# Normalisations of raw rows through a diagonal of row factors, chunk by chunk, and an attention pipeline one step deeper, in a two-block transformer kernel

## The reference

```python
def modulate(x, g, shift, scale):
    return rms_norm(x, g) * (1 + scale) + shift

h = modulate(x, lp["g_norm1"], sh1, sc1)
proj = h @ lp["w_in"]
...                       # two kinds of attention, a 2-D Fourier mix, sigmoid gates
x = x + gt1 * merge_branches(o_mla, o_gqa, o_four, proj[..., GATE_START:], lp)
x = x + gt2 * conv_ffn(modulate(x, lp["g_norm2"], sh2, sc2), lp)
```

## Time and profile before

| | us |
|---|---|
| median of 3 runs | 2947.84 (2944.81 to 2951.18) |
| profiled execution | 2950.79 |
| its span, first to last instruction | 2948.9 |
| TensorE busy | 2635.8 (89%) |
| VectorE busy | 1772.1 (60%) |
| ScalarE busy | 1445.4 (49%) |
| GpSimd busy | 631.0 (21%) |
| mean granted TensorE clock | 0.944 |

### The profile page before, as it was taken

How to read it: one execution, slowest core, us unless ns; L and a number is a source line. 1 busy time by engine, 2 the same in 40 slices (tenths; PEclk the granted TensorE clock), 3 DMA queues, 4 the chain that set the end, 5 groups by cost and what they waited for, 6 DMA issues and landing times.

```text
span 2948.9 us, 46949 instructions
## 1 busy us (share of the span) xinstructions
PE 2635.8 (89%) x17262; PEld 2293.7 (78%) x17262; DVE 1772.1 (60%) x2449; ACT 1445.4 (49%) x2194; POOL 631.0 (21%) x446
## 2 busy tenths in 40 slices
PE   5778998998998899769988999999799999988998
PEld 3547967987875799658667988978689789866996
DVE  5564756775674776657756765653556554455545
ACT  5453553663444376334444754444455454445544
POOL 0002203332211333231013323302023023111321
PEclk9787998998999999879998999999999999999999
DMA  8674514554540455434314656555246546532663
GB/s 298 205 255 125 159 58 143 170 173 130 174 129 14 138 172 185 121 97 141 104 56 127 188 187 192 187 178 179 85 125 195 173 157 188 191 129 75 183 195 126
DMA packets 332941, 450.47 MB, mean 153 GB/s; under 512 B 28192, under 2 KB 207392, under 8 KB 332768
## 3 DMA queue, kind: packets, MB, share of 16 engines
q1 hardware_dynamic: 332400, 446.58, 48.4%
q0 software_dynamic: 368, 1.57, 0.2%
HBM read 446.99 MB, written 1.05 MB: 152 GB/s over the span
## 4 chain that ended last, share of the span: by engine, by line
PE 78%; DVE 9%; ACT 5%; DMA 4%; issue 3%; POOL 1%; SPq 1%; DVEq 0%; ACTq 0%
PE S L780 24%; PE S L771 21%; PE G L780 14%; PE G L771 9%; DMA raw<-in_w_mod 4%; PE TB L828 3%; DVE wlo L574 2%; ACT whi L569 2%; PE S L857 2%; PE G L899 1%; ACT pp L1142 1%; POOL rs L1763 1%; DVE nmx L1552 1%; PE G L928 1%; PE S L928 1%
## 5 line engine op out<-in xcount | busy, mean ns | idle before, releaser
L574 DVE TENSOR_TENSOR wlo<-raw,whi 128x1024 fp32r<-128x1024 f32 x723 | 942.8, 1312 | 824.6 <-ACT whi L569 818.8
L569 ACT CAST whi<-raw 128x1024 fp32r<-128x1024 f32 x872 | 905.4, 1049 | 894.9 <-PE S L771 301.5
L780 PE MATMUL S<-hhi,whi 128*128 128x256 f32 x1952 | 547.3, 280 | 3.4 <-DVE wlo L574 1.6
L780 PE MATMUL S<-hhi,wlo 128*128 128x256 f32 x1952 | 546.5, 280 | 0.0
L780 PE MATMUL S<-hlo,whi 128*128 128x256 f32 x1952 | 546.2, 280 | 0.0
L574 POOL TENSOR_TENSOR wlo<-raw,whi 128x1024 fp32r<-128x1024 f32 x149 | 362.4, 2432 | 746.0 <-ACT whi L569 745.1
L780 PEld LDWEIGHTS S<-hhi,whi 128*128 128x128 f32 x1952 | 367.0, 188 | 5.3 <-issue 4.8
L780 PEld LDWEIGHTS S<-hlo,whi 128*128 128x128 f32 x1952 | 367.4, 188 | 0.2
L780 PEld LDWEIGHTS S<-hhi,wlo 128*128 128x128 f32 x1952 | 367.3, 188 | 0.0
L780 PE MATMUL G<-hhi,whi 128*128 128x256 f32 x1088 | 309.4, 284 | 16.7 <-DVE hlo L1279 15.0
L780 PE MATMUL G<-hlo,whi 128*128 128x256 f32 x1088 | 308.1, 283 | 0.0
(11 more groups left out here) (323 smaller groups left out, 4528.2 us busy)
## 6 DMA issues: line engine op xcount, KB each, us to landing
raw<-in_ffn_wi SPq DMA_DIRECT2D x352, 256.0 KB, 3.5
raw<-in_w_up SPq DMA_DIRECT2D x264, 256.0 KB, 3.3
raw<-in_w_mod SPq DMA_DIRECT2D x192, 256.0 KB, 3.7
raw<-in_w_in SPq DMA_DIRECT2D x192, 256.0 KB, 3.1
raw<-in_ffn_wo SPq DMA_DIRECT2D x160, 256.0 KB, 3.5
raw<-in_w_down SPq DMA_DIRECT2D x120, 256.0 KB, 3.3
raw<-in_a_wqkv SPq DMA_DIRECT2D x72, 256.0 KB, 3.0
raw<-in_w_o SPq DMA_DIRECT2D x48, 256.0 KB, 3.3
```

The lines of the kernel that those rows point to most:

```text
L569: act.copy(whi[:, n0 % SPLIT], raw[:, n0 % RAW]).then_inc(hi_done, 1)
L574: eng.tensor_tensor(wlo[:, n0 % SPLIT], raw[:, n0 % RAW], whi[:, n0 % SPLIT].bitcast(F32), ALU.subtract)\
L780: mm = pe.matmul(out_[:, m * T:(m + 1) * T], w, x, start=first and c == 0 and m == 0 and z == 0, stop=last and c == kc - 1 and z == len(te ...
```

## The change

The normalisations no longer scale rows before they are transposed. TensorE multiplies raw tiles of `resid` with a 128x128 diagonal of the row factors (`turn_rows`), which transposes and scales at once, into four banks. ScalarE takes out every chunk with scale and shift (`modulated`), VectorE does both parts of every split (`split_chunks`); `in` and the `up` of the first block wait for their chunks by twos. The squares are taken by ScalarE: over whole rows ahead of `in`, over half rows inside `wo1`. Where a `norm` follows a `down` (twice: latent 1 in layer 0, context 1 in layer 1), its whole work stands inside the second unit of that `down`: squares at slots 0 and 1, powers at 2, diagonals at 4, turning behind slots 5 to 8, modulating and splitting at slots 7 to 10. In attention the transposes follow three steps behind the scores (`TURN_LAG`), and the values of one step, 128 columns, four behind (`VALUE_LAG`); there are still three `prob` tiles.

```diff
-WARM_STEPS, WARM_PRODUCTS = 0, 6
+TURN_LAG, VALUE_LAG = 3, 4
...
+        def inner(st):
+            z = STAGES[STAGES.index(st) + 1] if st.kind == "down" and st.conv else None
+            return z if z and z.kind == "norm" else None
...
+        def split_with_norm(st, k, j, i, split, hooks):
+            for h in range(len(slot_shapes(st.kc))):
+                split(k, j, i, (h,))
+                if k == 1 and h in hooks:
+                    hooks[h]()
...
-            return st.kind in ("qkv", "pgate") or st.kind == "up" and not st.conv
+            return st.kind in ("in", "qkv", "pgate", "up")
...
+            def turn_rows(st, n):
+                pe.wait_ge(diag_done, NT * (st.ng + 1))
+                if n == 2:
+                    for b in range(2):
+                        wait_count(pe, bank_free[b], st.u + 2 - PAIRS)
+                for c in range(2):
+                    c0 = (2 * n + c) * P
+                    for t in range(NT):
+                        mm = pe.matmul(turned_banks(st)[n][:, c * T + t * P:c * T + (t + 1) * P], resid[st.s][:, t, c0:c0 + P],
+                                       diag2[:, t, :], start=True, stop=True, skip_group_check=True)
+                mm.then_inc(turned_done, 1)
...
+                        if st.kind == "down" and inner(st) and k == 1 and h in (5, 6, 7, 8):
+                            turn_rows(inner(st), h - 5)
...
-                for s in range(n + 3):
+                for s in range(n + VALUE_LAG):
                     if s < n:
                         scores(s)
...
-                    if 2 <= s < n + 2:
-                        turn(s - 2)
-                    if s >= 3 and s % 2 == 0:
-                        values((s - 4) // 2)
+                    if TURN_LAG <= s < n + TURN_LAG:
+                        turn(s - TURN_LAG)
+                    if s >= VALUE_LAG:
+                        values(s - VALUE_LAG)
...
-                    pe.wait_ge(rows_ready, st.rr + 2)
-                    for n in range(KD // 2):
-                        transposes(st.tk + n, [xn[:, t, c * P:(c + 1) * P] for c in (2 * n, 2 * n + 1) for t in range(NT)])
-                    wait_operand(st)
+                    if not inside(st):
+                        for n in range(KD // 2):
+                            turn_rows(st, n)
...
+            def row_squares(st, t):
+                act.activation(xn[:, t, :], resid[st.s][:, t, :], ACT.Square, scale=D ** -0.5,
+                               accum_out=ssq[:, t, 2:3]).then_inc(sq_done, 1)
+            def modulated(st, c):
+                scale, shift = modulation(st, c)
+                act.wait_ge(turned_done, st.nt + c // 2 + 1)
+                act.activation(unsplit[:, c, :], turned_banks(st)[c // 2][:, c % 2 * T:(c % 2 + 1) * T], ACT.Identity,
+                               scale=scale, bias=shift).then_inc(chunk_done, 1)
...
+                elif st.kind == "wo1":
+                    def half_squares(k, j, i):
+                        for b in range(2):
+                            act.wait_ge(half_ready, 4 * wo1s.index(st) + 2 * k + b + 1)
...
+                    hooks = {0: lambda: row_squares(z, 0), 1: lambda: row_squares(z, 1), 7: lambda: two(0),
+                             8: lambda: two(1), 9: lambda: two(2), 10: lambda: two(3)}
...
+            def row_diag(st, t):
+                dve.wait_ge(rs_ready, st.rq + t + 1)
+                dve.tensor_scalar(diag2[:, t, :], ident, rs[:, t, 0:1], None, ALU.mult).then_inc(diag_done, 1)
+            def split_chunks(st, n):
+                for c in (2 * n, 2 * n + 1):
+                    dve.wait_ge(chunk_done, norms.index(st) * KD + c + 1)
+                    dve.tensor_copy(hhi[:, c, :], unsplit[:, c, :]).then_inc(hhi_done, 1)
+                    dve.wait_ge(hhi_done, 2 * st.nt + c + 1)
+                    dve.tensor_tensor(hlo[:, c, :], unsplit[:, c, :], hhi[:, c, :].bitcast(F32), ALU.subtract).then_inc(hlo_done, 1)
...
-                        dve.tensor_tensor_reduce(scratch[:, :], x[:, t, :], x[:, t, :], 1.0 / D, EPS, ALU.mult, ALU.add,
-                                                 ms[:, t, 0:1]).then_inc(ms_ready, 1)
...
-                        dve.tensor_scalar(xn[:, t, :], x[:, t, :], rs[:, t, 0:1], None, ALU.mult).then_inc(rows_ready, 1)
...
+                        hooks = {2: pair(row_mean), 4: pair(row_diag), 7: lambda: split_chunks(z, 0), 8: lambda: split_chunks(z, 1),
+                                 9: lambda: split_chunks(z, 2), 10: lambda: split_chunks(z, 3)}
```

More of the change, by code:

```diff
@@ L529, in build, with inside, modulation @@
         last1 = [st for st in STAGES if st.kind == "down" and st.conv][-1]
+        wo1s = [st for st in STAGES if st.kind == "wo1"]
+        norms = [st for st in STAGES if st.kind == "norm"]
+        wides = [st for st in STAGES if st.kind == "up" and not st.conv]
+        def inner(st):
+            z = STAGES[STAGES.index(st) + 1] if st.kind == "down" and st.conv else None
+            return z if z and z.kind == "norm" else None
+        def inside(st):
+            return inner(STAGES[STAGES.index(st) - 1]) is st
+        def modulation(st, c):
+            w = int(st.which) - 1
+            return amul[:, st.l, w, c, st.s:st.s + 1], modT[:, st.l, 3 * w * KD + c, st.s:st.s + 1]
         def lo_by_pool(st, n0):
@@ L606, in turned @@
             outs = []
[L607 to L612, removed]
+            if st.kind == "ctrans":
                 outs = [(unsplit[:, c, :], col(f"gc{st.l}", c), None) for c in range(5 if st.full else 2)]
@@ L645, in parts_of @@
         def parts_of(st):
-            if st.kind not in ("norm", "ctrans"):
+            if st.kind != "ctrans":
                 return {}
@@ L1073, in _ @@
                             hi_operand(st, *split[q])
+                if st.kind == "norm" and not inside(st):
+                    if st.which == "1":
+                        for t in range(NT):
+                            row_squares(st, t)
+                    for c in range(KD):
+                        modulated(st, c)
                 if st.kind == "norm2":
@@ L1625, in gated @@
                             add = dve.tensor_tensor(x, x, tmp, ALU.add)
-                            if st is last1 and k == 1:
+                            if st.kind == "wo1":
+                                add.then_inc(half_ready, 1)
+                            elif st is last1 and k == 1:
                                 add.then_inc(rows_ready, 1)
@@ L1757, in _, with powers @@
                     pool.dma_start(pT[:, :, :, :], dram["pT"].rearrange("p (l c t) -> p l c t", l=DEPTH, c=2)).then_inc(ld_mask, 16)
-                for t in range(st.counts["rq"]):
+                def powers(st, t):
                     pool.wait_ge(ms_ready, st.rq + t + 1)
@@ L1763, in _ @@
                     pool.tensor_tensor(rs[:, t, w0:w0 + w], ms[:, t, w0:w0 + w], mhalf[:, 0:w], ALU.pow).then_inc(rs_ready, 1)
+                if not (st.kind == "norm" and inside(st)):
+                    for t in range(st.counts["rq"]):
+                        powers(st, t)
                 if st.counts["n"]:
@@ L1784, in _ @@
                                     lambda *at_: None, lambda *at_: None, chunks_lo)
+                    elif inner(st):
+                        z = inner(st)
+                        over_units(pool, st, lambda k, j, i: split_with_norm(
+                            st, k, j, i, lambda k, j, i, which: split_weights(st, j, i, k, lo, which),
+                            {2: lambda: [powers(z, t) for t in range(NT)]}))
                     else:
```

151 lines of the change are left out of this document (87 added, 64 removed).

## The result

The changed kernel takes 2862.1 us (median of four runs, 2859.0 to 2865.6) where the kernel before takes 2947.2: ratio 0.971, 95% interval 0.9694 to 0.9727, 2.9% less. Forecast were 2867 us, with a range of 2850 to 2897. The profiled execution took 2865.6 us (span 2863.8) against 2950.8 before, so 85.2 us went; 81.2 were forecast.

A forecast was written before the change was run, and what follows sets the result against it. TensorE, with 78% of the chain of waits, was taken to bound the kernel. 22.2 + 11.7 + 29.8 + 17.5 = 81.2 us off the profiled 2950.8 leaves 2869.6, or 2867 us against the median; range 2850 to 2897.

The forecast's parts named there:

- Outer normalisations: Normalisations 1, 2, 4, 6 and 7, outside a down projection: shorter stretches and a faster clock win 22.2 + 11.7 us.
- 12.5 of clock: Products right behind the outer normalisations no longer run at half clock: 7.7 us in 2, 4, 7 and 4.8 in 1, 6.
- the powers stay: In normalisations 2, 4, 7 GpSimd's two powers keep their 2.49 us; TensorE begins at 5.4 us instead of 7.2.
- Inner ones: Normalisations 3 and 5, moved inside a down projection: 13.3 and 16.5 us won, together 29.8.
- the queue on VectorE: Behind normalisation 3, chunks, weight subtractions and gated adds queue up, making a weight slot of the next product late: 2.6 us.
- that slot is GpSimd's own: 0.4: Behind normalisation 5 the fourth weight slot of the next product is GpSimd's, so only 0.4 us is lost.
- Attention: Turning one step deeper, values in halves: two latent stages win 12.7 us, dilated 2.3, window 2.0, context 0.5; 17.5 together.
- One: Outer normalisations: turning out of a standstill keeps the clock at 1.2 GHz; they give 18 instead of 34, 2883 us; chance 0.16.
- Two: VectorE late by the port lock: some 8 us in the down units, 1 in each outer normalisation; 2880 us; chance 0.12.
- Three: Attention gives nothing, as exponentials wait for the turning of three steps before: price 17.5, 2885 us; chance 0.12.
- four: Attention slower: a loop over one step makes wide steps 6.7 us instead of 3.9, 112 us more, 2997; chance 0.02.
- Five: Inner turning waits for its diagonal in the down unit: two more slots in each, 11 us, 2878 us; chance 0.02.

The follow-up runs named there:

- changed_again: The changed kernel unaltered, run once more beside later follow-up runs: 2859.9 us, ratio 0.9701 to the kernel before.
- wait_all: The changed kernel, but the product behind a first-block normalisation waits for all eight chunks, not two at a time: 2889.4 us, ratio 0.9808.
- attn_only: The kernel before with only the attention part of the change: 2928.3 us, ratio 0.9917.
- act_early: The changed kernel; behind an inner normalisation ScalarE waits for the gated products only ahead of its first evacuation, not its first weight split: 2861.6 us, ratio 0.9701.
- norm_only: The changed kernel with the old attention pipeline: 2888.9 us, ratio 0.9791 to the kernel before.
- transposed: The changed kernel with rows turned by transposes, one instruction for two, row factors left out of the result: 2851.9 us, ratio 0.9671.

## Why the prediction was right, and where not

**Outer normalisations**, 33.9 us forecast: 76.9 - 48.7 = 28.2 of stretches and the forecast 12.5 of clock, 40.7. The clock came back inside the turning as argued from the earlier trace rows. Mis-sized was TensorE's beginning: in 2, 4 and 7, 5.4 us was put for "the powers stay", with their 2.49 us, and it is 4.2. That duration came from the work beside them: begun at 486.71 in normalisation 2, two such powers would end at 489.2, and they end at 488.15. In 1 and 6, 4.9 and 4.1 were put, and it is 4.3 and 3.2. All this is worth 5.1 of the 6.8 us, a shorter turning (28.6 for 30.3) the rest.

**Inner ones**, 29.8 forecast: 16.9 + 18.0 + 4.9 of clock, less two turnings of 3.6 and the stalls of 2.7 and 2.9, 27.0. Behind 3 the queue on VectorE was forecast to 0.1 us (2.6), in part by luck: the 0.53 us that its subtraction then waited for ScalarE's split, in the row at 696.33, was not in the sum. Behind 5 the step "that slot is GpSimd's own: 0.4" failed: GpSimd was free, but its subtraction follows ScalarE's split, and ScalarE waited 3.99 us at the stage's start. The prediction had no term for that wait: it went by ScalarE's 1.75 us of idle time a slot.

**Attention**, 17.5 forecast, 19.5 measured. Latent 6.8 and 8.5 for 6.4 each (8.4 and 8.5 by changed_again); dilated 4.1 for 2.3, its wait for tiles 5.9 now 3.0. Window 0.6 for 2.0: it was put down as like the dilated one, but in the kernel before TensorE waited for its tiles only once there, 1.3 us. Context lost 0.5 where 0.5 was forecast as won: with no gap to fill, 64 more instructions are 1.5 us more of busy TensorE at the same clock of 1.00.

Together 40.7 + 27.0 + 19.5 = 87.2 for 85.2 measured; the 2.0 lie within what two executions differ by. The errors were +6.8, -2.8 and +2.0: that the total is nearer than its first term is luck.

**The rivals.** One (clock stays low): out by the windows at 1.00; wait_all shows what it would have looked like. Two (VectorE late by the port): its mechanism is there and makes the stalls together with the queue, but at 5.6 us where the forecast had 3.0, not with another 8 on top. Three and four (attention gives nothing, or a closed loop): out by attn_only. The sum of four turns its sign at 1.6 us per wide step (63 us over 40 steps), not at the 2.5 it gives. Five (the inner turning late): out; it costs 3.6 us.

## What to carry to other kernels

A duration read beside another engine's work is a duration of the pair: before a small operation is carried over into the sum for a changed kernel, look at what ran beside it and whether that stays. A wait that an engine makes at a stage's start hides what it could have done first, and when it is moved, ask what the released work will run beside: in act_early it met VectorE on their common port, and the stall only moved. After a standstill the first work of TensorE bought the clock back here, and a pause behind it of 2.6 us or more lost it again in four cases of five (wait_all); what lets a product begin on its first chunks was worth 27 us by the profiled spans and 29.5 by the medians.

## What the runs showed of the hardware that was not expected

A context stage of attention shows a granted clock of 1.00 in some profiled executions and 0.92 in others, with the same instructions: 38.3 us in the changed kernel and 40.6 in changed_again, 40.8 in attn_only; with the old attention 37.8 in the kernel before and 40.3 in norm_only. Why it falls in one and not in the other, no run here tells; at 2 us it is of the size of the differences that the last edits were after.

Sixteen fp32 transposes brought the clock from 0.50 to 1.00 nearly as well as products did (in transposed, and in normalisations 4 and 5 of the kernel before), and 3.2 to 5.3 us of standing behind a turning took it down again (wait_all). A power of GpSimd on 128 single values took 0.56 us alone and, beside VectorE's row work, 2.49 for two.
